# A two-layer hybrid decoder trunk: 18 of 22 tile pairs of the up projection as seven products of halves instead of eight, with weight sums on GpSimd

## What is computed

```python
def conv_ffn(h, w_up, conv_w, conv_b, w_down):
    S = h.shape[1]
    u = h @ w_up
    gate, val = jnp.split(u, 2, axis=-1)
    gp = jnp.pad(gate, ((0, 0), (CONV_W - 1, 0), (0, 0)))
    gate_c = conv_b + sum(conv_w[j] * gp[:, j:j + S] for j in range(CONV_W))
    return (jax.nn.silu(gate_c) * val) @ w_down
```

## Time and profile before

| What | us |
|---|---|
| Median of 3 runs | 1092.82 |
| Lowest, highest | 1092.51, 1094.67 |
| Profiled execution: span from its first to its last instruction | 1091.2 |
| TensorE matmuls busy | 1082.8 |
| TensorE weight loads busy | 907.6 |
| VectorE busy | 539.4 |
| ScalarE busy | 428.5 |
| GpSimd busy | 50.3 |
| Mean granted TensorE clock | 0.999 |

### The profile page before, as it was taken

How to read it: one execution, slowest core, us unless ns; L and a number is a source line. 1 busy time by engine, 2 the same in 40 slices (tenths; PEclk the granted TensorE clock), 3 DMA queues, 4 the chain that set the end, 5 groups by cost and what they waited for, 6 DMA issues and landing times.

```text
span 1091.2 us, 14756 instructions
## 1 busy us (share of the span) xinstructions
PE 1082.8 (99%) x5526; PEld 907.6 (83%) x5526; DVE 539.4 (49%) x809; ACT 428.5 (39%) x747; POOL 50.3 (5%) x51
## 2 busy tenths in 40 slices
PE   9999999999999999999999999999999999999998
PEld 8888888798888888888889987789888888888886
DVE  7544578654443434333366587664343434523344
ACT  6511456543232323222355377753323232422242
POOL 1100211000000000000000024200000000000000
PEclk9999999999999999999999999999999999999999
DMA  9332327333423232122272542122333333313231
GB/s 286 108 106 81 113 86 228 73 107 88 115 77 114 78 115 77 38 97 96 96 193 58 152 100 78 20 78 87 106 87 106 89 103 93 99 35 98 95 137 77
DMA packets 154821, 111.10 MB, mean 102 GB/s; under 512 B 35536, under 2 KB 140144, under 8 KB 154784
## 3 DMA queue, kind: packets, MB, share of 16 engines
q1 hardware_dynamic: 153776, 107.41, 33.4%
q0 software_dynamic: 864, 2.92, 0.9%
q10 hardware_dynamic: 144, 0.26, 0.1%
HBM read 106.87 MB, written 2.13 MB: 100 GB/s over the span
## 4 chain that ended last, share of the span: by engine, by line
PE 96%; DVE 2%; SPq 1%; ACT 0%; issue 0%; DMA 0%; DVEq 0%
PE ps L1555 18%; PE ps L1556 18%; PE ps L1557 18%; PE ps L1802 7%; PE ps L1803 7%; PE ps L1804 7%; PE ps L1747 2%; PE ps L1749 2%; PE ps L1748 2%; PE ps L1636 1%; PE ps L1638 1%; PE ps L1637 1%; PE ps L1897 1%; PE ps L1928 1%; PE ps L1910 1%; SPq L429 1%
## 5 line engine op out<-in xcount | busy, mean ns | idle before, releaser
L1555 PE MATMUL ps<-act_hi,w_hi 128*128 128x512 f32 (+1 forms) x1016 | 368.8, 363 | 1.8 <-DVE act_lo L1015 1.7
L1556 PE MATMUL ps<-act_lo,w_hi 128*128 128x512 f32 (+1 forms) x1016 | 366.4, 361 | 0.0
L1557 PE MATMUL ps<-act_hi,w_lo 128*128 128x512 f32 (+1 forms) x1016 | 366.4, 361 | 0.0
L1555 PEld LDWEIGHTS ps<-act_hi,w_hi 128*128 128x128 f32 x1016 | 191.7, 189 | 33.3 <-DVE act_lo L1015 2.1
L1556 PEld LDWEIGHTS ps<-act_lo,w_hi 128*128 128x128 f32 x1016 | 191.8, 189 | 29.0 <-issue 0.2
L1557 PEld LDWEIGHTS ps<-act_hi,w_lo 128*128 128x128 f32 x1016 | 191.7, 189 | 29.1
L1802 PE MATMUL ps<-w_hi 128*128 128x512 f32 x288 | 112.0, 389 | 0.0
L1803 PE MATMUL ps<-w_lo,w_hi 128*128 128x512 f32 x288 | 112.0, 389 | 0.0
L1804 PE MATMUL ps<-w_hi,w_lo 128*128 128x512 f32 x288 | 112.0, 389 | 0.0
L789 ACT ACTIVATE arena<-ps,vecs 128x512 f32<-128x512 f32 x44 | 34.3, 780 | 188.6 <-PE ps L1557 188.6
L1317 DVE SCALAR_TENSOR_TENSOR arena<-ps,vecs,arena 128x511 f32<-128x511 f32 x44 | 33.0, 750 | 144.4 <-ACT arena L789 144.4
(11 more groups left out here) (212 smaller groups left out, 1217.0 us busy)
## 6 DMA issues: line engine op xcount, KB each, us to landing
raw<-in_f_w_up SPq DMA_DIRECT2D x88, 512.0 KB, 4.6
raw<-in_f_w_down SPq DMA_DIRECT2D x44, 512.0 KB, 3.4
raw<-in_m_w_in SPq DMA_DIRECT2D x23, 512.0 KB, 4.3
raw<-in_m_w_out SPq DMA_DIRECT2D x8, 512.0 KB, 3.4
raw<-in_a_w_in SPq DMA_DIRECT2D x16, 256.0 KB, 4.7
raw<-in_a_w_out SPq DMA_DIRECT2D x16, 256.0 KB, 4.8
h<-in_x SPq DMA_DIRECT2D x4, 512.0 KB, 7.7
h<-in_x_turned SPq DMA_DIRECT2D x3, 512.0 KB, 7.0
```

What stands on the lines that cost most here:

```text
L1555: nc.tensor.matmul(dst, uh[:, k], zh, start=(k == 0), stop=False)
L1556: nc.tensor.matmul(dst, uh[:, k], zl, start=False, stop=False)
L1557: ins = nc.tensor.matmul(dst, ul[:, k], zh, start=False, stop=(k == KT - 1))
```

## The change

Write the k dimension of a product in two halves (512 rows each) and the tokens in two halves (256 each). A pair of tiles, gate and value, is then a 2 x 2 block times a 2 x 2 block: eight products of a half tile with a half of the activations. Strassen's scheme (in Winograd's form, with sums that build on one another) does it with seven products, of sums of the blocks:

- Pairs 0 to 3 of each layer (PLAIN = 4) stay as they were; pairs 4 to 21 (18 a layer, 36 in all) take the new form.
- **Activations**: once a layer VectorE makes four sums of quarters of the activations (T1 to T4, 8 additions of 1024 elements in `first_sums` and `last_sums`, from high and low parts), and ScalarE and VectorE split them (`form_hi`, `form_lo`, 4 of 1024 each). They lie in free space of the arena, in the buffers of the norm gains, and in a new one.
- **Weights**: for each pair GpSimd makes four sums of halves (`weight_sums`, 128 x 512 each, both inputs in SBUF). A pair has seven forms of half size instead of four: value (two halves) and the second half of gate from `raw`, and the four sums. ScalarE rounds them (`raw_hi` twice: 1024 and 512 elements; `sum_hi` twice: 1024 each), VectorE makes the low parts (`raw_lo`, `sum_lo`, the same sizes). Sums lie where their low parts go.
- **Products**: each is 4 steps of k x 3 matmuls of 256 columns. Products 3, 4, 5 and 7 add on to what an earlier one left in the same half bank. Before TensorE goes on adding, ScalarE copies that intermediate state out (`part`, four of 256 elements a pair), and VectorE adds the parts up (`gate_first`, `gate_last`, `val_first`, 256 elements each). The conv follows as before (`joined_conv`, the taps, SiLU, the gating product). The value's first half is made in banks 6 and 7.
- **Order**: ScalarE's and VectorE's loops interleave the parts and joins of pair f with the weights of pair f + 1 (before: the pair two ahead). TensorE waits for `part_done` ahead of products 3, 4, 5 and 7, and for `f_lo` and `w_lo_done` ahead of 1, 2 and 5. The down projection takes the blocks in the order 2, 0, 3, 1.
- GpSimd's scratch for the descriptors of its own DMAs shrinks (`dynamic_dma_scratch_size=4096`), which makes room in SBUF.

The diff cut to its core, with the common indentation taken off; the allocation of buffers and semaphores is left out.

```diff
+    PLAIN = 4
+    SEVENS = FT - PLAIN
+    HT = S // 2
+    QW = KT // 2 * P
...
-    FFN_SLOTS = [4 + n % 4 for n in range(2 * FT)] + [n % 2 for n in range(FT - TAIL)]
+    FFN_SLOTS = [4 + n % 4 for n in range(2 * PLAIN)]
+    FFN_SLOTS += [(0, 1, 6, 7)[n % 4] for n in range(2 * SEVENS)] + [n % 2 for n in range(FT - TAIL)]
...
+        for l in range(2):
+            if g >= G_DOWN[l]:
+                users.append(G_DOWN[l] - (1 if SLOT[g] >= 4 else 3))
...
+    def weight_sums(l, m, t):
+        up, n = G_UP[l], l * SEVENS + t - PLAIN
+        gate, val = raw[:, 2 * t], raw[:, 2 * t + 1]
+        lo = sums[:, t]
+        first, last = slice(0, QW), slice(QW, 2 * QW)
+        for q in range(2):
+            pool.wait_ge(raw_in[2 * t + q], m * 16 + landed(up + 2 * t + q))
+        pool.wait_ge(w_used, m * 4 + counted(up + 2 * t - 3))
+        nc.gpsimd.tensor_tensor(lo[:, 5], gate[:, first], gate[:, last], ALU.add).then_inc(s_sum, 1)
+        pool.wait_ge(s_sum, m * 8 + 4 * n + 1)
+        nc.gpsimd.tensor_tensor(lo[:, 4], lo[:, 5], val[:, first], ALU.subtract).then_inc(s_sum, 1)
+        nc.gpsimd.tensor_tensor(lo[:, 3], val[:, first], gate[:, first], ALU.subtract).then_inc(s_sum, 1)
+        pool.wait_ge(s_sum, m * 8 + 4 * n + 2)
+        nc.gpsimd.tensor_tensor(lo[:, 6], val[:, last], lo[:, 4], ALU.subtract).then_inc(s_sum, 1)
+    def ffn_sums(l):
+        with pool.Fori(PLAIN // 2, FT // 2) as m:
+            for t in range(2):
+                weight_sums(l, m, t)
+    ffn_sums(0)
     s = SLOT[G_AIN + 2]
     pool.wait_ge(w_hi_done, G_AIN + 3)
     pool.wait_ge(w_lo_done, counted(G_AIN + 1))
...
+    def raw_hi(m, t, last):
+        g = up + 2 * t + (0 if last else 1)
+        act.wait_ge(raw_in[2 * t + (0 if last else 1)], m * 16 + landed(g))
+        act.wait_ge(w_used, m * 4 + counted(up + 2 * t - 3))
+        hi = forms_hi[t]
+        if last:
+            ins = nc.scalar.copy(hi[:, 2], raw[:, 2 * t, QW:])
+        else:
+            ins = nc.scalar.copy(hi[:, 0:2].rearrange("p a c -> p (a c)"), raw[:, 2 * t + 1])
+        ins.then_inc(f_hi, 1)
+    def sum_hi(m, t, j):
+        n = l * SEVENS + t - PLAIN
+        act.wait_ge(s_sum, m * 8 + 4 * n + 3 + j)
+        fs = slice(3 + 2 * j, 5 + 2 * j)
+        ins = nc.scalar.copy(forms_hi[t][:, fs], sums[:, t, fs])
+        if j == 0:
+            ins.then_inc(f_hi, 1)
+        else:
+            ins.then_inc(w_hi_done, 2)
+    def part(m, t, r):
+        n = l * SEVENS + t - PLAIN
+        act.wait_ge(product_mm, m * 12 + 6 * n + (1, 2, 3, 5)[r])
+        src = ps[:, 2 * t, 0:HT] if r == 1 else ps[:, 2 * t + 1, HT:]
+        dst = first_part[:, t] if r == 0 else parts[:, r - 1]
+        nc.scalar.copy(dst, src).then_inc(part_done, 1)
...
+    def joined_conv(m, t):
+        n = l * SEVENS + t - PLAIN
+        f = m * 2 + t
+        act.wait_ge(joined, m * 6 + 3 * n + 2)
+        nc.scalar.activation(cv[:, t], ps[:, 2 * t], ACT.Identity,
+                             scale=taps[l][:, 2, bass.ds(f, 1)],
+                             bias=taps[l][:, 3, bass.ds(f, 1)]).then_inc(cv0, 1)
+        act.wait_ge(cv2, m * 2 + (l * FT + t + 1))
+        nc.scalar.activation(cv[:, t], cv[:, t], ACT.Silu).then_inc(silu_done, 1)
+    def seven(m, t, nm, nt):
+        part(m, t, 0)
+        if nt is None:
+            split_hi(down)
+        else:
+            raw_hi(nm, nt, False)
+        part(m, t, 1)
+        if nt is not None:
+            raw_hi(nm, nt, True)
+        part(m, t, 2)
+        if nt is None:
+            split_hi(down + 1)
+        else:
+            sum_hi(nm, nt, 0)
+            sum_hi(nm, nt, 1)
+        part(m, t, 3)
+        if nt is None:
+            for j in range(2):
+                nc.scalar.copy(hid_pair[j][0], hid[:, j]).then_inc(hid_hi, 1)
+        joined_conv(m, t)
     nc.scalar.preload_act_table(ACT.Silu)
     if l == 0:
         act.wait_ge(vec_in, 16)
-    with act.Fori(0, FT // 2 - 1) as i:
-        conv(i, 0)
-        hi_pair(i, 2)
-        conv(i, 1)
-        hi_pair(i, 3)
-    for j in range(2):
-        split_hi(down + j)
-    for j in range(2):
-        nc.scalar.copy(hid_pair[j][0], hid[:, j]).then_inc(hid_hi, 1)
-    conv(FT // 2 - 1, 0)
-    conv(FT // 2 - 1, 1)
+    conv(0, 0)
+    hi_pair(0, 2)
+    conv(0, 1)
+    hi_pair(0, 3)
+    for j in range(4):
+        form_hi(j)
+    conv(1, 0)
+    raw_hi(PLAIN // 2, 0, False)
+    raw_hi(PLAIN // 2, 0, True)
+    sum_hi(PLAIN // 2, 0, 0)
+    sum_hi(PLAIN // 2, 0, 1)
+    conv(1, 1)
+    with act.Fori(PLAIN // 2, FT // 2 - 1) as m:
+        seven(m, 0, m, 1)
+        seven(m, 1, m + 1, 0)
+    seven(FT // 2 - 1, 0, FT // 2 - 1, 1)
...
+    def conv(i, t, join=None):
...
+            join()
         dve.wait_ge(silu_done, i * 2 + n)
...
+    def first_sums():
+        if l == 0:
+            dve.wait_ge(z_lo, NB - FIRST_MOVED)
+            dve.wait_ge(moved_lo, FIRST_MOVED)
+        else:
+            dve.wait_ge(t_lo, len(TURNS))
+            dve.wait_ge(moved_lo, len(MOVED))
+        nc.vector.tensor_tensor(t3, h1b, l1b, ALU.add)
+        link(nc.vector.tensor_tensor(t4, h0b, l0b, ALU.add))
+        link(nc.vector.tensor_tensor(t1, t4, h0a, ALU.subtract))
+        nc.vector.tensor_tensor(t1, t1, l0a, ALU.subtract).then_inc(t_sum, 1)
+        dve.wait_ge(t_sum, 4 * l + 1)
+    def last_sums():
+        nc.vector.tensor_tensor(t2, t3, t1, ALU.subtract).then_inc(t_sum, 1)
+        dve.wait_ge(t_sum, 4 * l + 2)
+        nc.vector.tensor_tensor(t3, t3, t4, ALU.subtract).then_inc(t_sum, 1)
+        dve.wait_ge(t_sum, 4 * l + 3)
+        link(nc.vector.tensor_tensor(t4, h1a, t2, ALU.subtract))
+        nc.vector.tensor_tensor(t4, t4, l1a, ALU.add).then_inc(t_sum, 1)
+        dve.wait_ge(t_sum, 4 * l + 4)
+    def form_lo(j):
+        dve.wait_ge(t_form_hi, 4 * l + j + 1)
+        nc.vector.tensor_tensor(t_lo_form[j], t_sums[j], t_hi_form[j].bitcast(F32),
+                                ALU.subtract).then_inc(t_form_lo, 1)
...
+            flat = [w[:, 0:2].rearrange("p a c -> p (a c)") for w in (lo, hi)]
+            ins = nc.vector.tensor_tensor(flat[0], raw[:, 2 * t + 1], flat[1].bitcast(F32), ALU.subtract)
+        ins.then_inc(f_lo, 1)
+    def sum_lo(m, t, j):
+        n = l * SEVENS + t - PLAIN
+        if j == 0:
...
+        fs = slice(3 + 2 * j, 5 + 2 * j)
+        lo, hi = forms_lo[t][:, fs], forms_hi[t][:, fs]
+        ins = nc.vector.tensor_tensor(lo, sums[:, t, fs], hi.bitcast(F32), ALU.subtract)
+        if j == 0:
+            ins.then_inc(f_lo, 1)
+        else:
+            ins.then_inc(w_lo_done, 2)
+    def gate_first(m, t):
+        n = l * SEVENS + t - PLAIN
+        dve.wait_ge(product_mm, m * 12 + 6 * n + 4)
+        dve.wait_ge(part_done, m * 8 + 4 * n + 3)
+        nc.vector.tensor_tensor(ps[:, 2 * t, 0:HT], ps[:, 2 * t, 0:HT], parts[:, 1], ALU.add)\
+            .then_inc(joined, 1)
+    def gate_last(m, t):
+        n = l * SEVENS + t - PLAIN
+        dve.wait_ge(part_done, m * 8 + 4 * n + 4)
+        nc.vector.tensor_tensor(ps[:, 2 * t, HT:], parts[:, 0], parts[:, 2], ALU.add)\
+            .then_inc(joined, 1)
+    def val_first(m, t):
+        n = l * SEVENS + t - PLAIN
+        dve.wait_ge(w_used, m * 4 + counted(up + 2 * t + 1))
+        nc.vector.tensor_tensor(ps[:, 2 * t + 1, 0:HT], ps[:, 6 + t, 0:HT], first_part[:, t], ALU.add)\
+            .then_inc(joined, 1)
+        dve.wait_ge(joined, m * 6 + 3 * n + 3)
+    def seven(m, t, nm, nt):
+        if nt is None:
+            split_lo(down)
+        else:
+            raw_lo(nm, nt, False)
+            raw_lo(nm, nt, True)
+        gate_first(m, t)
+        if nt is None:
+            split_lo(down + 1)
+        else:
+            sum_lo(nm, nt, 0)
+        gate_last(m, t)
+        if nt is None:
+            for j in range(2):
+                lo_hid(j)
+        else:
+            sum_lo(nm, nt, 1)
+        conv(m, t, lambda: val_first(m, t))
+    first_sums()
+    conv(0, 0)
+    lo_pair(0, 2)
+    conv(0, 1)
+    lo_pair(0, 3)
+    last_sums()
+    for j in range(4):
+        form_lo(j)
+    conv(1, 0)
+    raw_lo(PLAIN // 2, 0, False)
+    raw_lo(PLAIN // 2, 0, True)
+    sum_lo(PLAIN // 2, 0, 0)
+    sum_lo(PLAIN // 2, 0, 1)
+    conv(1, 1)
+    with dve.Fori(PLAIN // 2, FT // 2 - 1) as m:
+        seven(m, 0, m, 1)
+        seven(m, 1, m + 1, 0)
+    seven(FT // 2 - 1, 0, FT // 2 - 1, 1)
+    seven(FT // 2 - 1, 1, None, None)
...
-    with pe.Fori(1, FT // 2) as i:
+    for n in range(2, PLAIN):
+        t = n % 2
+        pe.wait_ge(hid_done, l * FT + n + 1)
+        for q in range(2):
+            pe.wait_ge(w_lo_done, counted(up + 2 * n + q))
+            project(4 + 2 * t + q, 2 * t + q).then_inc(w_used, 1)
...
+    def product(t, form, z, bank, ts, start):
+        dst = ps[:, bank, ts]
+        for k in range(KT // 2):
+            cs = slice(k * P, (k + 1) * P)
+            uh, ul = forms_hi[t][:, form, cs], forms_lo[t][:, form, cs]
+            zh, zl = z[k]
```

(35 more changed lines are left out.)

74 lines of the change are left out of this document (58 added, 16 removed).

## The result

The changed kernel takes **1061.58 us** (median of 4 runs, 1060.85 to 1063.61) against 1092.73 of the kernel before on the same chip: ratio 0.9715, interval 0.9702 to 0.9729. The profiled execution has a span of 1060.2 us against 1091.2: 31.0 less, where 18.1 less were forecast.

The account below looks back on a forecast made before the run. TensorE's matmuls, covering 1082.8 of 1091.2 us, were taken as the bound. Terms: -28.8 (shorter products) + 9.7 (waits) + 1.0 (edges) = -18.1 us, so 1074.7 us for the median, range 1063 to 1092.

Parts of the forecast that it names:

- TensorE's new work: Up loops: 84 matmuls of 256 columns replace 48 of 512, 10.08 us a pair for 10.88, 28.8 us less.
- What a pair asks of the others: New loop: VectorE 7.8 us, ScalarE 6.8, GpSimd 5.1 a pair; by sums alone all fit in 10.08.
- The lock: VectorE ops with two SBUF inputs and GpSimd ops reading SBUF exclude each other; together 9.9 of 10.08 us a pair.
- The chain: GpSimd's sums through VectorE and ScalarE to the seventh product: 9.2 us, where it should start at 8.64.
- 0.27 us of wait a pair: TensorE's wait ahead of the seventh product, between ends of 0 and 0.6; over 36 pairs 9.7 us given back.
- case (a): Rival for the new loop: the lock costs nothing, TensorE steps through 84 x 0.120 unbroken, 1065 us; chance 0.27.
- The edges: Around the new loops: `first_sums` 0.6 us late, low parts of pair 4's sums 0.5 us a layer; 1.0 in all.
- the end, the loads and the scratch: Last gating before the down projection and weight loads cost nothing; smaller GpSimd DMA scratch 0 to 2 us, taken as 0.
- Rival (c): GpSimd's chain becomes the period, with `sum_hi` 1 ahead of `part` 3; slower than before, 1116 us; chance 0.16.
- My expectation for experiment 2: An extra sum, 1.26 us less 0.74 of slack plus some 0.1, gives about 0.6 us a pair: 1083 us.

Follow-up runs that it names:

- experiment 5: Changed kernel with only the buffer `t_last` moved up by 64 bytes: 1064.82 us, ratio 0.9733.
- experiment 8: Kernel before the change, with its up loop in 256-column matmuls, all else the same: 1118.36 us, ratio 1.0222.
- experiment 1: Changed kernel with three of GpSimd's four weight sums replaced by memsets to 1.0 that read nothing: 1061.21 us, ratio 0.9703.
- experiment 2: Changed kernel with GpSimd making its first weight sum twice, the extra one into an unused slot: 1102.67 us, ratio 1.0081.
- experiment 9: Changed kernel with activations and all four activation sums at 192 bytes modulo 256 from the weights: 1059.22 us, ratio 0.9692.
- experiment 11: Changed kernel with only the activation sums T1 to T4 moved to 192 bytes modulo 256 from the weights: 1056.37 us, ratio 0.9665.
- experiment 7: Kernel before the change, with `act_hi` and `act_lo` at 64 bytes modulo 256 from the weights: 1099.26 us, ratio 1.0050.
- experiment 10: Kernel before the change, with `act_hi` and `act_lo` at 192 bytes modulo 256 from the weights: 1105.77 us, ratio 1.0120.
- experiment 4: Changed kernel with the buffers of T1 and T4 swapped, so product 5 reads `t_last` and product 4 doesn't: 1062.95 us, ratio 0.9717.
- experiment 6: Changed kernel with activations and `t_last` at 64 bytes modulo 256 from the weights, T1 to T3 at 128: 1061.71 us, ratio 0.9703.

## Why the prediction was wrong, point by point

- **TensorE's new work, -28.8 us: right.** Steps of 0.120, measured in the loop and by experiments 5 and 8.
- **What a pair asks of the others: right**, with sums of 1.33 us beside 1.27 forecast.
- **The lock: it exists, as read** from the earlier trace rows (experiment 1 takes it away and the ops shrink back).
- **The chain: the step that failed**, "VectorE's `raw_lo` pair, which comes due in the middle (about 3.7 us in, behind ScalarE's first rounding) and goes ahead of the fourth sum, 1.22 + 0.69". It does come due in the middle (3.4 us after the pair before ends), but one op of it passes, in 1.08 us, and then the fourth sum has its turn. Sums and row together: 6.16 us for 5.1 + 0.1 + 1.75 = 6.95, 0.79 less. The handoffs were estimated long too: 0.25 for 0.4 at the start, 0.06 for 0.3 back to TensorE, and 0.12 less over the three small terms (0.09, 0.96 and 0.36). In all the seventh product is possible 7.88 us into the pair instead of 9.18, against 8.56 that TensorE needs. So "0.27 us of wait a pair" was 0, and 9.7 us too much stood in the sum. Either error by itself would have been enough to make a wait out of none: 0.27 is less than the 0.69 of the op that did not go ahead, and less than the 0.51 of the handoffs and small terms. The earlier trace rows were read as "VectorE's ops in a row don't let GpSimd in between"; that was one place, with another kind of op on GpSimd, and I made it the rule. Had the chain been taken with the fourth sum ahead (a wait of 0), case (a) would have followed.
- **The edges, 1.0 us: 0.8 measured**, in layer 0 alone. It is `part` 0 and not the low parts of the sums of pair 4, which I had named: the step of the wait was wrong, its size nearly right. `first_sums` are hidden, as said, and so are the end, the loads and the scratch.
- **Beyond every case: -2.9 us** from the place of `t_last`. Case (a) gave 1065, and the kernel of experiment 5, without this, takes 1064.8. The 1.4 us by which the range was missed are of this kind: I had allowed a step of 256 columns one duration, as all showed it.
- **Rival (c)** was rightly built but had a cushion of 0.68 us a pair instead of none. As its price I had 0.4 us a pair for each 0.1 us on each sum; what experiment 2 shows is that a whole sum more lengthens the chain by 1.70, and costs that less the cushion.

My expectation for experiment 2 failed by the same misreading as the forecast: a sum added was priced as its own length, and not with the extra turn that it gives to VectorE.

**Still open.** First, who comes next at the lock. The event of the earlier trace rows is no accident: it is in the trace of every run here, 2.84 or 2.85 us long, in the changed kernel too:

```profile
166.91 0.69 DVE L1366 TENSOR_TENSOR act_lo<-arena,act_hi 128x512 fp32r<-128x512 f32 x1 [0.66 <-ACT act_hi L757]
167.29 2.84 POOL L594 TENSOR_SCALAR arena<-arena,hn_half 128x256 f32<-128x256 f32 x1 [5.75 <-ACT arena L775]
167.51 2.35 DVE L1103 TENSOR_TENSOR w_lo<-raw,w_hi 128x1024 fp32r<-128x1024 f32 x2
```

GpSimd's op waits there for the end of one VectorE op and for two more that began after it: neither turns nor first come, first served. It is a tensor_scalar with one input in SBUF and per-partition scalars, the sums are tensor_tensor; whether that makes the difference no run shows. Second, why the step depends on the distance, and why 192 gives two values. In the first pairs of experiment 9's loops every product that no wait touches takes 1.36 us (113 ns a step); after a wait ahead of product 3 (in pair 7 of layer 0 and pair 5 of layer 1) all take 1.41 (118) to the end of the loop, with no further wait. In experiment 11 products 4 and 5 go to 1.41 behind the longer ones of these waits, and come back. What a wait changes there isn't shown.

## What to carry to other kernels

When two engines share a lock, follow the order op by op. Where they take turns, as the sums and low parts did here, an engine's chain grows by one op of the other for each of its own that finds the other waiting, and a cushion of some tenths of a us a pair decides between nothing and 40 us. But don't take the order from another pair of ops: the earlier trace rows and the new loop show two different ones. Write down the slack of every wait, since the next gain uses up the smallest (experiment 11). Put helper work on the engine that has room, even at twice the time per op, as long as it isn't on the way to the bound. And where a loop is bound by matmuls, look at the step of each operand's buffer by itself: a shift of the four sums to a distance of 192 bytes was worth 5.2 us here, and the lock at most 0.8.

## What the runs showed of the hardware that was not expected

- **Turns at the lock.** A GpSimd sum of 512 elements and a VectorE subtraction alternate while both stand: in 34 of 36 pairs of the changed kernel (means of 2223, 1762 and 1718 ns for 1.33, 1.22 and 0.69 alone), and twice a pair in 33 pairs of experiment 2. GpSimd's tensor_scalar of the earlier trace rows doesn't: VectorE's next two ops pass it, in every run. Once it has the lock, an op takes 0.1 to 0.2 us less than alone (1.08, 1.15, 0.55). The Trainium skill (SBUF — State Buffer, "Who interferes with whom") has the lock and that it is exclusive, and the trace agrees; who comes next is what the rows add.
- **The step of a matmul depends on the distance of its moving operand from its weights.** With 256 columns 120 ns at a distance from the weights of 0 modulo 256 bytes, 117 to 118 at 64, 117 to 120 at 128, 113 to 118 at 192; with 512 columns, in `project`, 227 ns at 0, 226 to 232 at 64 and 233 to 234 at 192. All at a granted clock of 1.00. That it is the distance and not the place alone is shown by the output projection of experiments 7 and 10, the rest of the pattern by experiments 4 to 7 and 9 to 11; its cause is not.
- **The 13 ns by which two steps of 256 columns exceed one of 512** held in every loop with operands at 0, and at 192 they are gone (2 x 113 against 233).
